# Where the scan's read-outs stand on TensorE, and which engine copies its last states

## What is computed

```python
z = rmsnorm(x) @ w_in                      # 2048 -> 5120
q, k, v, u, h, gb, gc = split(z)
o_att = attend(q, k, v)                    # prompt: on itself; samples: on a cache of 2048 rows and 8 new ones
# diagonal complex state space: 32 groups of 16 channels, 64 complex states each
x_re, x_im = u @ bb_re, u @ bb_im          # the scan's projections
h_re, h_im = scan over time of a * h + x   # samples start from a given state
y = h_re @ c_re - h_im @ c_im + d * u      # the scan's read-out, then GELU and a gate
out_state = h[:, -1]                       # last state of the prompt and of each sample
x = x + concat(norm(o_att), norm(y), norm(conv)) @ w_out
x = x + (silu(xn @ w_gate) * (xn @ w_up)) @ w_down
```

## Time and profile before

| | |
|---|---|
| median of 3 executions | 1514.79 us (1514.79 to 1515.89) |
| the profiled execution: its own time | 1514.19 us |
| its span, first to last instruction | 1512.4 us |
| TensorE busy | 1484.1 us (98%) |
| VectorE busy | 841.8 us (56%) |
| ScalarE busy | 609.1 us (40%) |
| GpSimd busy | 218.7 us (14%) |
| granted TensorE clock, mean | 0.998 |

### The profile page before, as it was taken

How to read it: one execution, slowest core, us unless ns; L and a number is a source line. 1 busy time by engine, 2 the same in 40 slices (tenths; PEclk the granted TensorE clock), 3 DMA queues, 4 the chain that set the end, 5 groups by cost and what they waited for, 6 DMA issues and landing times.

```text
span 1512.4 us, 27919 instructions
## 1 busy us (share of the span) xinstructions
PE 1484.1 (98%) x11367; PEld 1418.4 (94%) x11367; DVE 841.8 (56%) x1093; ACT 609.1 (40%) x947; POOL 218.7 (14%) x317
## 2 busy tenths in 40 slices
PE   9999999999999999999999999999999999999997
PEld 9999777878777999999999999999999999999997
DVE  7669899974577677444445445445444433343334
ACT  6333444547556353333333333333333333334332
POOL 7864244400630000000000000000000000000100
PEclk9999999999999999999999999999999999999999
DMA  7556798999897444444444444444444444444442
GB/s 269 182 169 217 277 373 321 352 386 370 310 337 282 156 152 143 151 153 150 144 150 153 149 144 150 153 147 145 151 152 147 147 152 153 146 149 153 147 151 106
DMA packets 93270, 296.39 MB, mean 196 GB/s; under 512 B 9728, under 2 KB 11008, under 8 KB 92800
## 3 DMA queue, kind: packets, MB, share of 16 engines
q1 hardware_dynamic: 92608, 294.10, 57.4%
q10 hardware_dynamic: 576, 1.08, 0.2%
HBM read 289.06 MB, written 5.43 MB: 195 GB/s over the span
## 4 chain that ended last, share of the span: by engine, by line
PE 82%; DVE 11%; ACT 3%; POOL 2%; issue 2%; DMA 0%; DVEq 0%; ACTq 0%
PE ps L2096 20%; PE ps L2094 20%; PE ps L2095 20%; PE ps L1940 3%; DVE wlo L1061 3%; PE ps L1978 2%; PE ps L1984 2%; PE ps L1979 2%; PE ps L1942 2%; PE ps L1787 1%; PE ps L1793 1%; PE ps L2047 1%; PE ps L2045 1%; PE ps L2046 1%; DVE tm L1150 1%
## 5 line engine op out<-in xcount | busy, mean ns | idle before, releaser
L1417 DVE TENSOR_TENSOR wlo<-raw,whi 128x1024 fp32r<-128x1024 f32 x264 | 325.2, 1232 | 519.9 <-ACT whi L938 519.8
L938 ACT ACTIVATE whi<-raw 128x1024 fp32r<-128x1024 f32 x264 | 279.9, 1060 | 606.2 <-PE ps L2096 601.7
L2096 PE MATMUL ps<-xh,wlo 128*128 128x320 f32 x1400 | 432.6, 309 | 0.0
L2094 PE MATMUL ps<-xh,whi 128*128 128x320 f32 x1400 | 432.6, 309 | 0.0
L2095 PE MATMUL ps<-xl,whi 128*128 128x320 f32 x1400 | 432.6, 309 | 0.0
L2095 PEld LDWEIGHTS ps<-xl,whi 128*128 128x128 f32 x1400 | 262.8, 188 | 0.0
L2096 PEld LDWEIGHTS ps<-xh,wlo 128*128 128x128 f32 x1400 | 262.8, 188 | 0.0
L2094 PEld LDWEIGHTS ps<-xh,whi 128*128 128x128 f32 x1400 | 262.8, 188 | 0.0
L2094 PE MATMUL ps<-hh,whi 128*128 128x320 f32 x696 | 215.1, 309 | 0.0
L2095 PE MATMUL ps<-hl,whi 128*128 128x320 f32 x696 | 215.1, 309 | 0.0
L2096 PE MATMUL ps<-hh,wlo 128*128 128x320 f32 x696 | 215.1, 309 | 0.0
(11 more groups left out here) (336 smaller groups left out, 1832.1 us busy)
## 6 DMA issues: line engine op xcount, KB each, us to landing
raw<-in_w_gu SPq DMA_DIRECT2D x176, 512.0 KB, 3.7
raw<-in_w_dn SPq DMA_DIRECT2D x88, 512.0 KB, 3.7
raw<-in_w_in SPq DMA_DIRECT2D x78, 512.0 KB, 5.2
kv<-in_cv SPq DMA_DIRECT2D x64, 512.0 KB, 6.9
kv<-in_ck SPq DMA_DIRECT2D x32, 768.0 KB, 7.1
kv<-in_ck SPq DMA_DIRECT2D x32, 512.0 KB, 7.2
raw<-in_w_out SPq DMA_DIRECT2D x32, 512.0 KB, 3.8
raw<-in_cv SPq DMA_DIRECT2D x16, 512.0 KB, 8.0
```

The source lines that it names most:

```text
L938: act.activation(whi[:, j % SPL, :], raw[:, j % RAW, :], ACT.Copy).then_inc(S["w_hi"], 1)
L1417: v.tensor_tensor(wlo[:, j % SPL, :], raw[:, j % RAW, :], whi[:, j % SPL, :].bitcast(F32), ALU.subtract) \
L2094: t_.matmul(out, whi[:, slot, w], ah[:, k, :], start=(k == 0), stop=False)
L2096: last = t_.matmul(out, wlo[:, slot, w], ah[:, k, :], start=False, stop=(k == 2 * units - 1))
```

## The change

The second and third read-outs go from bank 7 to bank 5, and all four go from `middle` of one slot to `end` of the slot before, ahead of what stood there. The place of VectorE's `scan_output` stays. The copies to `ho` and the two memsets go from VectorE to ScalarE, each as an ACTIVATE with Copy; the memsets become copies from a stretch of `mask_new` that holds the same negative number. In part 4 of the scan VectorE still waits for its own `ssm_h`, and from tile 4 on it also waits for `state_done` of four tiles before.

```diff
-        def y_bank(it):
-
-            return 7 if it in (1, 2) else 5
...
             for i in range(ST):
-                if scan_slot(i, 4) + 2 == s and i % 4 == 3:
-                    middle.append((y_bank(i // 4), ("y", i // 4)))
+                if scan_slot(i, 4) + 1 == s and i % 4 == 3:
+                    end.append((5, ("y", i // 4)))
...
+            def states(i):
+
+                act.wait_ge(S["ssm_h"], i + 1)
+                act.activation(ho[:, :, i, :], hbs[i % 4][:, :, SEQ - 1:NT:DEC_SEQ], ACT.Copy).then_inc(S["state_done"], 1)
...
+            def no_new(b):
+
+                if b:
+                    act.wait_ge(S["p_turned"], b)
+                else:
+                    act.wait_ge(S["mask_in"], 32)
+                    act.wait_ge(S["early_done"], 1)
+                for q, at in ((slice(32, 64), 32) if b < 4 else (slice(0, 32), 0), (slice(64, P), 0)):
+                    never = mask_new[q, at:at + 32].rearrange("p (a n) -> p a n", a=1).to_broadcast([q.stop - q.start, 4, 32])
+                    act.activation(sall[q, :, KQ:KW], never, ACT.Copy).then_inc(S["no_new"], 1)
...
             def exponent(b, groups):
                 act.wait_ge(S["s_bias"], 4 * b + 4)
+                act.wait_ge(S["no_new"], 2 * b + 2)
...
+                if s == START_OF[0] - 3:
+                    no_new(0)
+                for b in batches(s, TURN + 1):
+                    if b + 1 < DEC_BATCH:
+                        no_new(b + 1)
...
+                    if scan_slot(i, 4) + 1 == s:
+                        states(i)
...
-                dve.wait_ge(S["p_turned"], b + 1)
-                if b < DEC_BATCH - 1:
-                    no_new((slice(32, 64), slice(64, P)) if b + 1 < 4 else (slice(0, 32), slice(64, P)))
...
                 if part == 4:
                     if i >= 4:
                         dve.wait_ge(S["c_done"], i // 4 * 4)
+                        dve.wait_ge(S["state_done"], i - 3)
...
                     dve.wait_ge(S["ssm_h"], i + 1)
-                    v.tensor_copy(ho[:, :, i, :], h[:, :, SEQ - 1:NT:DEC_SEQ]).then_inc(S["state_done"], 1)
...
-                if s == START_OF[0] - 3:
-                    dve.wait_ge(S["early_done"], 1)
-                    no_new((slice(32, 64), slice(64, P)))
...
             def middle(s):
 
-                for i in range(3, ST, 4):
-                    if scan_slot(i, 4) + 2 == s:
-                        read_out(i)
...
+                for i in range(3, ST, 4):
+                    if scan_slot(i, 4) + 1 == s:
+                        read_out(i)
                 for step in range(KS):
                     for b in batches(s, step):
                         scores(b, step)
```

More of the change, by code:

```diff
@@ L347, in build @@
         den_ready den_turned sin_ready sin_done bt_ready bt_done bt_moved c_ready early_done keep_ready
-        q_zero q_ready k_used s_masked s_max s_spread s_top s_bias p_exp p_turned new_masked vn_zero
+        q_zero q_ready k_used s_masked s_max no_new s_spread s_top s_bias p_exp p_turned new_masked vn_zero
         p_sums s_sum s_inv v_used vn_done vn_moved
@@ L1112, in maxima @@
                 v.tensor_reduce(sbias[0:32, 4:8], quads[0:32].rearrange("p j g -> p g j"), AX.X, ALU.max).then_inc(S["s_top"], 1)
-            def no_new(quadrants):
-                for q in quadrants:
-                    step(v.memset(sall[q, :, KQ:KW], NEG))
             def turn_probabilities(b):
@@ L1193, in scan_output @@
                 dve.wait_ge(S["c_done"], 4 * it + 4)
-                v.scalar_tensor_tensor(out=z[:, ZU + it, :], in0=z[:, ZU + it, :], scalar=vec[:, V_D + it:V_D + it + 1], in1=ps[:, y_bank(it), 0:NT],
+                v.scalar_tensor_tensor(out=z[:, ZU + it, :], in0=z[:, ZU + it, :], scalar=vec[:, V_D + it:V_D + it + 1], in1=ps[:, 5, 0:NT],
                                        op0=ALU.mult, op1=ALU.add).then_inc(S["y_acc"], 1)
@@ L1759, in read_out @@
                     pe.wait_ge(S["c_ready"], 1)
-                fill(y_bank(i // 4), "y", i // 4)
+                fill(5, "y", i // 4)
                 for plane in range(2):
@@ L1763, in read_out @@
                         q = slice(32 * (j % 4), 32 * (j % 4) + 32)
-                        last = t_.matmul(ps[q, y_bank(i // 4), 0:NT], cmat[:, plane, j, :], h[:, plane], start=(plane == 0), stop=(plane == 1),
+                        last = t_.matmul(ps[q, 5, 0:NT], cmat[:, plane, j, :], h[:, plane], start=(plane == 0), stop=(plane == 1),
                                          tile_position=(0, 32 * (j % 4)))
```

## The result

| | before | changed kernel |
|---|---|---|
| median of the runs | 1514.86 us (1514.79 to 1515.89, 4 runs) | 1528.55 us (1527.64 to 1528.85, 4 runs) |
| ratio to before | | 1.0088, 95% interval 1.0074 to 1.0101 |
| profiled execution: time, span | 1514.19, 1512.4 us | 1528.7, 1526.9 us |

The change costs 13.7 us by the medians, 14.5 between the two profiled executions. The forecast of 1523.8 us was 8.9 over the median of before, and the range ended at 1527.0, 1.55 short of the result. The direction and the place of the loss were right, the size was not.

What follows compares the result with a forecast made beforehand. TensorE was taken to bound the kernel (busy 98% of the span), with VectorE setting the pace in the changed stage. Slot terms of +7.6 us and +2.0 for one clock fall on 1514.2 gave 1523.8 us, range 1518.5 to 1527.

Steps and rivals of the forecast that it cites:

- Slot 37, the mask waits, slot 62: TensorE's waits for masks shrink as VectorE saves work: -0.7 in slot 37, -0.6 slot 43, -0.9 around 55, -0.4 slot 62.
- ScalarE at nothing: ScalarE's 32 new copies, about 0.2 us each and 6.4 in all, fit its idle time and cost nothing.
- First read-out, +1.4: Moved from slot 39 to end of 38: TensorE arrives at 151.6, `h` is ready at 153.0, a new wait of 1.4 us.
- `scan_output` comes in time: Claim for the first read-out: bank 5 is read back early enough for the projection of tile 5.
- Second, +2.5: Moved from slot 50 to end of 49: waits of 2.6 for `h` and 5.6 for `scan_output`, less 5.7 gone.
- Third, +5.3: Moved from slot 58 to end of 57: no wait for `h`, but the projection of tile 13 waits 5.3 us for `scan_output`.
- Fourth, +1.0: Moved from slot 66 to end of 65: a wait for `h` between nothing and 1.4 us, taken as 1.0.
- The clock, +2.0 for one fall: TensorE's clock falls to half once after the new long waits, costing 2.0 us, with bounds of 0 to 4.
- The sum without the clock: All slot terms from the first to the fourth read-out, mask-wait savings included: +7.6 us.
- Rival B: Same waits for the reading of the read-out in slots 50 and 58, but the clock holds: 1521.8 us, chance 0.32.
- C: The wait in slot 58 does not appear because VectorE is earlier there: +2.3, 1516.5 us, chance 0.10.
- D: VectorE bounds the whole stage, TensorE's waits only shift, and 4.1 us come off the end: 1510.1 us, chance 0.06.

Runs made afterwards that it cites:

- the half alone: Kernel before with only the copies to `ho` and the memsets moved to ScalarE, read-outs in their old places and banks: 1512.33 us against 1514.78, ratio 0.9985.
- the run of the third read-out alone: Kernel before with only the read-out of tiles 8 to 11 moved to the end of slot 57 and into bank 5: 1522.02 us, ratio 1.0048.
- the fillers: Changed kernel plus 28 unneeded matmuls into free bank 6 ahead of each projection of tiles 9 and 13: 1523.67 us, ratio 1.0058.
- the two runs with fillers in slot 49: 16 unneeded matmuls ahead of the second read-out, added to the changed kernel with fillers before both projections (1523.47 us), or with `scan_output` early (1512.64 us).

## Why the prediction was wrong in size

- *Slot 37, the mask waits, slot 62.* Forecast -0.7, -0.6, -0.9 and -0.4; measured -0.77, -0.61, -0.96 and -0.53. The prices of a pair of memsets and a copy, and the slots in which they count, hold.
- *ScalarE at nothing.* Held: the half alone gives -2.5 us. A copy to `ho` took 0.24 us there (0.18 on VectorE) and a copy in place of a memset 0.31 (0.17), more than the 0.2 of the earlier trace rows; ScalarE's 7.2 us more are nearer to the 6.4 of the sum than to the 11 that the prediction gave beside it.
- *First read-out, +1.4.* Slots 38 and 39 came out at +2.1. The wait for `h` is 1.53 as forecast; the read-out ahead of the scores also makes `scan_output` late for the projection of tile 5, by 0.6, and "`scan_output` comes in time" was wrong.
- *Second, +2.5.* The waits are 3.0 and 4.7 us where 2.6 and 5.6 stood, but between them TensorE lost 1.5 at half speed, which came out of the second. Measured 4.47 + 1.52 = 6.0, less 2.6 for the half clock behind the second: +3.4. Of the 0.9 over the forecast some 0.5 is what remained of the half speed in slot 49.
- *Third, +5.3.* Wait 5.28; 1.08 + 6.87 less 2.7 for the clock is 5.25. Right, and the run of the third read-out alone agrees: a wait of 5.1, and 6.64 us from the projection to the next unit, so 1.07 + 6.27 less 2.3 for the clock is 5.0.
- *Fourth, +1.0.* Measured 2.95 - 1.22 = +1.7. That is over the upper bound of 1.4: the wait was 1.80.
- *The clock, +2.0 for one fall.* **This is the step that failed.** Two falls were paid for in full, and the fillers show them as 4.9 us; a third, in slot 49, left some 0.5. Two things were wrong in the step. It allowed for one fall where both long waits brought one, though the text named both as longer than the 3.8 us after which the clock fell at the end. And the price of one was taken as up to half of 4.2 us, from a single stretch of 4.23 us at the program's start; here the lower clock lasts 6.8 us, and what takes 4.31 us from the projection to the next unit at full speed took 6.94 and 7.05, so 2.6 and 2.7 each instead of 2.0. Two falls at 2.0 were inside the range (1525.8); their real price and the 2.0 us in waits below put the result outside.
- The sum without the clock was 7.6; without it the slots above, less 2.6 and 2.7 for the clock, give 9.6. Between the profiled executions 14.5 us were measured where 7.6 + 2.0 had been forecast, so 4.9 were missing: 9.6 - 7.6 = 2.0 in waits and 5.3 - 2.0 = 3.3 in the clock, less the 0.4 of small differences.
- *Rival B* (the clock holds) rested on one execution in which it held through 3.6 us. The second execution of the same kernel shows it falling at that very wait. One profile in which nothing happened was no evidence that nothing can; B's 0.32 was too high, and the range too narrow at its upper end. *C* and *D* fell: `scan_output` ended 4.7 and 5.3 us after TensorE had come.
- The Trainium skill (TensorE: Matmul & The Clock Gate, HAM oscillation), weighed in the prediction, says that a stream broken by long waits comes back at half clock after each. By that rule the forecast would have been 1514.2 + 7.6 + 4 = 1525.8, nearer to the result. These runs agree with it where TensorE waited 4.7 to 5.4 us with no filler: six such waits in four profiled executions, half speed behind all six.

## To carry to other kernels

When a producer is moved earlier, move its reader too: the bank that it fills is held until the reader, on another in-order engine, comes to its place, and whatever shares the bank waits behind it. Here the move of the read-outs cost 19.1 us by itself with the reader left, and won 2.8 with the reader one slot earlier and the producer behind the work that was ready (with ScalarE's copies, 13.7 lost and 6.3 won). Moving the producer was not needed for that: with ScalarE's copies, moving the reader of the second and third read-out alone won 5.9. Price a new long wait of TensorE with the half clock behind it (of the sixteen unfilled ones of 3.0 to 5.4 us here only one brought no fall), look whether a further wait swallows that price, and profile twice before saying that the clock holds.

## What the runs showed of the hardware

- The granted clock fell at waits of TensorE as short as 3.0 to 3.1 us (slot 49, in all five profiled executions in which it stood unfilled), and at one of 3.6 us in three of four: the earlier trace rows are the fourth. At 2.06 us in slot 65 it fell in one kernel, at 1.8 us in the changed kernel it did not, in either execution.
- A stretch at the lower clock lasted 3.4 or 6.8 us, and the same wait brought the one and the other in two executions of one kernel. It can also begin after TensorE has gone on, 1.6 us behind a wait of 3.5 us.
- Half speed is not a fixed price: 3.4 us of it made its own slots 1.3 to 1.6 us longer, of which by the slots some 0.5 remained, in the kernel before and in the two runs with fillers in slot 49; the rest was taken out of a later wait.
- Why one wait of 3.6 us brings the clock down and the next does not was not tested and stays open. The two behaviours were seen in one profiled execution each of the same kernel.
